# Branch norms and the pooling mixer interleaved with the last four units of the input projection and the first of the merge, in a streaming encoder step

## The reference

```
qa, ka, va, ub, cq, ckv, kpe, ud, gate_in = split_cols(h @ lw['w_in'])
q = (rmsnorm(cq, lw['c_q_norm']) @ lw['w_uq'])          # C: latent attention, query latent
ckv = rmsnorm(ckv, lw['c_kv_norm'])                     # C: key/value latent
ud = ud[..., :CONV_WIDTH] * jax.nn.sigmoid(ud[..., CONV_WIDTH:])
o_a = swa(qa, ka, va)                                   # A: sliding window attention
o_b = pool_mix(ub)        # B: trailing means over 2, 4, 8, 16 tokens, minus u, times w_pool, times a gain
o_c = mla(q, ckv, kpe)
o_d = silu(layernorm(conv31(ud)))                       # D: causal depthwise convolution of 31 taps
merged = sum over b of sigmoid(gate_b) * (o_b @ w_o_b)
x += merged @ w_out;  x += swiglu(rmsnorm(x))
```

## Time and profile before

| | us |
|---|---|
| median of 3 runs | 2405.38 (2404.38 to 2407.51) |
| profiled execution, its own time | 2410.11 |
| its span from the first to the last instruction | 2408.3 |
| PE busy (share) | 2270.8 (94%) |
| DVE, POOL, ACT busy | 1302.2, 949.3, 860.8 |
| mean granted TensorE clock | 0.981 of full |

### The profile page before, as it was taken

The page is one execution under the profiler, slowest core; times in us unless marked ns, Lnnn a source line. Parts: engine busy times, 40 slices in busy tenths (PEclk is TensorE's granted clock), DMA queues, the critical chain, the costliest instruction groups (busy, mean ns, idle before and its releaser), DMA issues.

```text
span 2408.3 us, 39646 instructions
## 1 busy us (share of the span) xinstructions
PE 2270.8 (94%) x14968; PEld 2179.9 (91%) x14968; DVE 1302.2 (54%) x2344; ACT 860.8 (36%) x1676; POOL 949.3 (39%) x988
## 2 busy tenths in 40 slices
PE   5997999999999999999989979999999989999996
PEld 5996999788999999999889969988889989999996
DVE  6996243333347835727389752533332487275364
ACT  2014333444314534526311152334442245254352
POOL 3552455232464332323445425542326623333331
PEclk9999999999999999999999989999999999999998
DMA  5241222011232221222224302211112312223221
GB/s 183 84 161 52 68 71 65 29 40 40 81 103 79 71 92 67 97 66 79 96 94 138 114 34 66 70 53 40 40 36 92 109 62 88 79 79 97 67 79 57
DMA packets 70417, 187.79 MB, mean 78 GB/s; under 512 B 19680, under 2 KB 22336, under 8 KB 69248
## 3 DMA queue, kind: packets, MB, share of 16 engines
q1 hardware_dynamic: 53536, 163.27, 20.7%
q10 hardware_dynamic: 16736, 22.52, 2.8%
HBM read 173.46 MB, written 14.14 MB: 78 GB/s over the span
## 4 chain that ended last, share of the span: by engine, by line
PE 87%; DVE 8%; issue 2%; ACT 2%; ACTq 0%; DMA 0%; SPq 0%; DVEq 0%
PE gemm L640 43%; PE gemm L1051 17%; PE gemm L1041 14%; PE side L1051 3%; PE side L924 2%; PE side L904 1%; DVE rstd L1607 1%; DVE act_lo L2034 1%; PE side L710 1%; PE side L855 1%; PE side L911 1%; DVE prod L1636 1%; DVE prod L1790 1%; PE side L782 1%; DVE x L1793 1%
## 5 line engine op out<-in xcount | busy, mean ns | idle before, releaser
L620 POOL TENSOR_TENSOR ring_lo<-w_raw,ring_hi 128x512 fp32r<-128x512 f32 x232 | 307.8, 1329 | 590.7 <-ACT ring_hi L1469 590.7
L603 POOL CAST w_hi<-w_raw 128x384 fp32r<-128x384 f32 x376 | 212.1, 564 | 803.1 <-PE gemm L640 783.7
L640 PE MATMUL gemm<-h_hi,w_hi 128*128 128x320 f32 x1728 | 431.2, 331 | 21.7 <-DVE h_lo L1613 17.0
L605 POOL TENSOR_TENSOR w_lo<-w_raw,w_hi 128x384 fp32r<-128x384 f32 x376 | 432.7, 1151 | 30.1
L640 PE MATMUL gemm<-h_hi,w_lo 128*128 128x320 f32 x1728 | 395.6, 310 | 0.0
L640 PE MATMUL gemm<-h_lo,w_hi 128*128 128x320 f32 x1728 | 395.5, 310 | 0.0
L640 PEld LDWEIGHTS gemm<-h_hi,w_hi 128*128 128x128 f32 x1728 | 294.3, 190 | 53.4 <-issue 39.5
L1051 PE MATMUL gemm<-act_hi,ring_hi 128*128 128x320 f32 x960 | 299.9, 312 | 18.9 <-issue 10.0
L1051 PE MATMUL gemm<-act_hi,ring_lo 128*128 128x320 f32 x960 | 299.1, 312 | 0.0
L1051 PE MATMUL gemm<-act_lo,ring_hi 128*128 128x320 f32 x960 | 299.0, 311 | 0.0
L640 PEld LDWEIGHTS gemm<-h_hi,w_lo 128*128 128x128 f32 x1728 | 290.6, 189 | 0.0
(11 more groups left out here) (276 smaller groups left out, 4168.8 us busy)
## 6 DMA issues: line engine op xcount, KB each, us to landing
w_raw<-in_ws_ff SPq DMA_DIRECT2D x120, 512.0 KB, 3.3
w_raw<-in_ws_gate SPq DMA_DIRECT2D x64, 512.0 KB, 3.3
w_raw<-in_ws_in SPq DMA_DIRECT2D x44, 512.0 KB, 3.3
w_raw<-in_ws_proj SPq DMA_DIRECT2D x64, 256.0 KB, 2.6
w_raw<-in_ws_out SPq DMA_DIRECT2D x16, 512.0 KB, 3.3
w_raw<-in_ws_fd SPq DMA_DIRECT2D x16, 384.0 KB, 3.0
x_park<-x ACTq DMA_DIRECT2D x2, 2560.0 KB, 12.7
x<-x_park ACTq DMA_DIRECT2D x4, 1280.0 KB, 5.8
```

Of the source, the lines that this page charges most:

```text
L603: eng.tensor_copy(w_hi[s][:, cols], w_raw[s][:, cols]).then_inc(w_high.sem, 1)
L605: eng.tensor_tensor(w_lo[s][:, cols], w_raw[s][:, cols], w_hi[s][:, cols].bitcast(F32), ALU.subtract).then_inc(w_split.sem, 1)
L620: eng.tensor_tensor(lo, src, hi.bitcast(F32), ALU.subtract).then_inc(lo_plain.sem, 1)
L640: mm = eng.matmul(dst[:, hf, 0:HALF], w, r[:, k, cols], start=first and k == 0 and part == 0, stop=last and k == kk - 1 and part == 2)
```

## The change

It moves the side work. TensorE's units 18 to 21 leave the loop and are written tile by tile, with the side work between tiles; DVE's and ACT's orders follow; the bank list changes with them. Pool scratch and the four pool results move to slices 2 to 7 of `macc` (the memory of x, which is parked in HBM by then), so that pool results no longer share `rstd` and the squares no longer share the partial sums' buffers. The seven stores move from ACT's queue to SP's, behind the cache loads and ahead of the load of unit 22. The core of the diff:

```
-        pw0p, pw1p, pws, pld = sq0, sq1, t2b, rstd
+        pws = t2b
+        pw0p, pw1p, pld = macc[:, 2, :], macc[:, 3, :], [macc[:, 4 + g, :] for g in range(4)]
 SyncE, after the load of kpe_cache, before the merge loads:
+                read_unit(eng, l, 16)
+                read_unit(eng, l, 17)
+                (five stores of kT, vT, kTs; two of k_full and v_full to o_k_s and o_v_s)
 TensorE:
-                with eng.Fori(1, A_UNITS // 2) as i:
+                with eng.Fori(1, A_UNITS // 2 - 2) as i:
-                colsum("lnm", [y[:, t, :] for t in range(4)], lambda n: None)
-                for g in range(4):
-                    ... pool product g ...
-                    merge_tiles(0, 2 * g, 2 * g + 2)
-                colsum("ckvn", *sq_tiles(0, 1), square=True)
-                colsum("lnv", *sq_tiles(1, 4), square=True)
-                colsum("cqn", *sq_tiles(5, 2), square=True)
-                merge_tiles(0, 8, 12)
-                merge_tiles(1, 0, 12)
+                unit_tiles(18, 0, KT)
+                unit_tiles(19, 0, 3)
+                evacuated(eng, l, ("conv", 3))
+                evacuated(eng, l, "convs")
+                for n in range(4):
+                    colsum("lnm", [y[:, t, :] for t in range(4)], n)
+                unit_tiles(19, 3, KT)
+                unit_tiles(20, 0, 1)
+                colsum("lnv", lnv, 0, 0)
+                colsum("lnv", lnv, 1, 0)
+                unit_tiles(20, 1, 3)
+                colsum("lnv", lnv, 2, 0)
+                unit_tiles(20, 3, 5)
+                colsum("lnv", lnv, 3, 0)
+                unit_tiles(20, 5, 7)
+                pool(0)
+                unit_tiles(20, 7, KT)
+                unit_tiles(21, 0, 3)
+                pool(1)
+                unit_tiles(21, 3, 6)
+                colsum("ckvn", sq_tiles(4, 1), 0, 4)
+                unit_tiles(21, 6, KT)
+                merge_tiles(0, 0, 5)
+                pool(2)
+                merge_tiles(0, 5, 7)
+                colsum("cqn", ..., 0, 5); colsum("cqn", ..., 1, 5)
+                merge_tiles(0, 7, 12)
+                merge_tiles(1, 0, 8)
+                pool(3)
+                merge_tiles(1, 8, 12)
 ScalarE, new order:
+   queries_out(0); squares of y 0, 1; queries_out(1); squares of y 2, 3; square of ckv;
+   stds("lnv"); pool(0); queries_out(2); square of cq 0; pool(1); four Silu and high parts;
+   queries_out(3); stds("ckvn"); square of cq 1; pool(2); merge_gate(0);
+   wait ckv_ready; stds("cqn"); store o_ckv; merge_gate(1); pool(3)
 VectorE, new order, behind the convolution:
+   pool(0); centre y 0 to 3; rotate kpe; pool(1); pool(2); reciprocal lnv; scale y 0 to 3;
+   o_lo 0 to 3; reciprocal ckvn, scale ckv; reciprocal cqn, scale cq 0, 1;
+   merge(0); pool(3); merge(1)
```

More of the change, by code:

```diff
@@ L70, in _bank_uses @@
     u += [(("lnm", h), 4 + h) for h in range(2)]
-    u += [(("pool", g, h), 6 + h) for g in range(4) for h in range(2)]
+    u += [(("lnv", h), 4 + h) for h in range(2)]
+    u += [(("pool", g, h), 6 + h) for g in range(2) for h in range(2)]
     u += [(("ckvn", h), 4 + h) for h in range(2)]
-    u += [(("lnv", h), 4 + h) for h in range(2)]
+    u += [(("pool", 2, h), 6 + h) for h in range(2)]
     u += [(("cqn", h), 4 + h) for h in range(2)]
+    u += [(("pool", 3, h), 6 + h) for h in range(2)]
     u += [(("kpe", h), 6 + h) for h in range(2)]
@@ L688, in _, with unit_tiles @@
                         products(l, i * 2 + s, G[s], s, KT, h_hi, h_lo)
+                def unit_tiles(u, first, last):
+                    for k in range(first, last):
+                        if k == 0:
+                            psum(u % 2, u // 2)
+                        product(l, u, G[u % 2], u % 2, k, KT, h_hi, h_lo)
                 def merge_tiles(n, first, last):
@@ L702, in merge_tiles @@
                             product(l, unit + 1, G[1], 1, t - KT, 4, o_hi, o_lo)
[L704 to L715, removed]
@@ L717, in sq_tiles, with colsum @@
-                def sq_tiles(first, n):
-                    return [sq[(first + k) % 2] for k in range(n)], \
-                        lambda k: eng.wait_ge(sq_ready.sem, sq_ready.at(l, first + k + 1))
+                def colsum(name, tiles, n, square=None):
+                    if square is not None:
+                        eng.wait_ge(sq_ready.sem, sq_ready.at(l, square + n + 1))
+                    for hf, cols in halves:
+                        if n == 0:
+                            fill(l, (name, hf))
+                        mm = eng.matmul(B[4 + hf][:, 0:HALF], ones[:, :], tiles[n][:, cols],
+                                        start=(n == 0), stop=(n == len(tiles) - 1))
+                        if n == len(tiles) - 1:
+                            mm.then_inc(side.sem, 1)
+                    if square is not None and n < len(tiles) - 1:
+                        mm.then_inc(sq_used.sem, 1)
@@ new lines, in sq_tiles, with pool @@
+                def sq_tiles(first, n):
+                    return [sq[(first + k) % 2] for k in range(n)]
+                def pool(g):
+                    eng.wait_ge(pooled.sem, pooled.at(l, g + 1))
+                    for hf, cols in halves:
+                        bank = fill(l, ("pool", g, hf))
+                        eng.matmul(bank[:, 0:HALF], wpl[:, g, :], pld[g][:, cols], start=True, stop=True)\
+                           .then_inc(side.sem, 1)
+                unit_tiles(18, 0, KT)
@@ L1234, in _, with queries_out @@
                 copy_unit(17, vT)
-                for t in range(4):
+                def queries_out(t):
                     g, free = take(18 + t)
@@ L1711, in _, with pool @@
                 eng.wait_ge(hist_zeroed.sem, hist_zeroed.at(l, 2))
-                step = 0
-                for g in range(4):
-                    src = (pbp[:, g, :], pbs[:, g, :, :])
+                eng.wait_ge(x_parked.sem, x_parked.at(l, 16))
+                def pool(g):
+                    step = sum(2 * (k + 1) + 3 for k in range(g))
+                    src, res = (pbp[:, g, :], pbs[:, g, :, :]), pld[g]
                     for lev in range(g + 1):
@@ L1755, in _ @@
                             ins.then_inc(ln_centred.sem, 1)
[L1757 to L1760, removed]
+                read_unit(eng, l, 13)
+                eng.tensor_tensor(kper[:, :], kper[:, :], cs[0:64, :], ALU.mult).then_inc(kpe_rot.sem, 1)
+                pool(1)
+                pool(2)
+                scaled(l, 1, lambda hf: ("lnv", hf))
                 for t in range(4):
```

95 lines of the change are left out of this document (50 added, 45 removed).

## The result

The changed kernel takes 2391.03 us (2388.87 to 2395.04, four runs), for 2405.53 (2404.38 to 2407.51) of the kernel before, timed beside it: a ratio of 0.9941, interval 0.9929 to 0.9954, or 14.5 us less. I had forecast 2388.5 and a gain of 16.9. The profiled execution took 2390.43 us, with a span of 2388.6.

The account below looks back on a forecast made before the run. TensorE bounds the kernel (87% of the chain), with 41.0 us wasted in two stretches. L745 at 77.5 instead of 85.0 and 86.9 gains 7.5 + 9.4 = 16.9: 2405.4 - 16.9 = 2388.5 us, range 2379 to 2400.

Parts of the forecast that it names:

- The convolution's end: After three tiles of unit 19, TensorE's LayerNorm sum waits for the convolution: a new stall of 2.0 us per layer.
- rival 2: More waits bite (cqn margin, clock at the convolution, lasting low clock): gain 5 to 9 us, 2398 us; chance 0.17.
- To the end of unit 22: TensorE's remaining tiles of units 19 to 22 and side work, up to merge 0's gate, end at 52.3 us.
- The chain to pool 3: From unit 22's end through ACT and DVE work: 16.4 us plus 2.1 of GpSimd contention, pool 3 ready at 70.9.
- The stall: TensorE runs out of tiles at 62.9 us and waits 8.0 us for pool 3 (5.9 to 9.8).
- The clock behind it: Lower TensorE clock after the wait for pool 3, up to L745: 2.0 us (bounds 0 and 4.6).
- To the rotary-key product: Pool 3's product 1.1 us, four tiles 3.5 and clock loss: L745 starts at 77.5 us after unit 18's start.
- The stores: SP issues seven stores in some 5 us before unit 22's load, issued near 169.6; 5 us slack, no cost taken.
- Rival 3: The stores choke the weights, so unit 22 comes late; at 20 us late, 2420 us; chance 0.07.
- Scratch in the accumulator: Removes the wait of pool g+1 for product g, letting DVE run ahead; its price is none.
- Rival 1: Stall at pool 3 much smaller, only the 2.0 us convolution wait left: gain 37.1 us, 2368 us; chance 0.1.
- rival 4: No change: the attention's first steps wait for cache loads or weights instead, within 0.2% of 2405; chance 0.06.

Follow-up runs that it names:

- filler: The changed kernel with 42 useless matmuls ahead of TensorE's wait for pool 3; 2387.52 us, ratio 0.9932.
- pool3_early: The changed kernel with DVE computing pool 3 ahead of the cq scaling instead of behind merge 0; 2391.24 us, ratio 0.9941.
- early_nolow: pool3_early without GpSimd's subtraction for the low weight parts, the high part multiplied instead (result not the reference's); 2374.77 us, ratio 0.9877.
- stores_act: The changed kernel with the seven stores back on ACT's queue, ahead of the copies of unit 18; 2394.03 us, ratio 0.9956.
- late_pool3: The changed kernel with TensorE's pool 3 multiplied behind the rotary-key product and first new-row transposes; 2375.71 us, ratio 0.9885.
- scratch_only: The kernel before with only pool scratch and results moved to the accumulator and its own wait removed, orders and stores unchanged; 2393.34 us, ratio 0.9961.

## Why the prediction was right, by its own steps

**The convolution's end: right in the wait, incomplete in its cost.** I forecast 2.0 us; 1.91 and 1.92 were measured. I gave the clock behind it no cost in the sum and put it into a rival. It falls in layer 1 of the changed kernel (6.24 us for 4.54, 1.7 us), in layer 1 of filler and of pool3_early, in layer 0 of early_nolow, in both layers of stores_act, and in neither of late_pool3. It is part of rival 2, and it is the term that the sum lacked.

**To the end of unit 22: right.** I forecast 52.3; ACT's sigmoid, released by it, starts at 209.57, which is 52.5. The thin margin at cqn held: no wait stands there.

**The chain to pool 3: right in its shape, one term wrong.** I forecast pool 3 ready at 70.9; it was ready at 69.9 (226.94). The term of 1.28 us for the sigmoid's table load behind the wait is wrong, since the load stands ahead of it. In the trace before it stood behind a wait for DVE, and I took that for a rule; this wait is for TensorE. Contention was forecast at 2.1 us and measured as 1.8 in pool 3 and 0.4 in cq's scaling, 2.2 together. The split of 235.74 that I cited for the reciprocal meets only its last tenth of a microsecond; that the reciprocal is untouched is shown by the changed kernel, where it takes 4.15 us (212.70) beside a subtraction of 1.02 us at 212.93.

**The stall: right.** I forecast 8.0 us (5.9 to 9.8) from 62.9 on; 6.91 and 6.97 were measured, from 63.1 on. Nearly all of the missing microsecond is the table load. late_pool3 shows that this wait and its clock are what separates 2391 from 2376, but for the 1.7 us of the convolution's clock in the profiled pair.

**The clock behind it: right in the mean.** I forecast 2.0 us; counted from 4.6 us for the product and four tiles at full speed it is 1.6 in layer 0 and 2.9 in layer 1, and filler takes it away.

**To the rotary-key product.** I forecast it at 77.5; it started at 76.1 and 79.2. Layer 0 is the table load and a smaller clock cost; layer 1 has 1.7 us from the convolution and 1.3 more behind pool 3. The two gains are 16.6 us together, for 16.9. That this is so close is partly luck. Layer 0 gained 1.4 us more than forecast and layer 1 1.7 less, from terms that have nothing to do with each other: a table load counted that wasn't there, a clock cost at the convolution left out. And the larger gain that I forecast for layer 1 rested on its longer stretch before (86.9 for 85.0 us), which was longer chiefly because the clock fell at the variance sum in that layer alone, 3.0 us (see scratch_only).

**The stores: right that they cost nothing, the working off.** SP's issues took 8.4 us and not 5, and the load of unit 22 went at 172.55 instead of 169.6; the slack of 5 us that I had estimated took it, as the wait at 182.63 shows. Rival 3 is refuted by stores_act.

**Scratch in the accumulator: priced wrongly as a step.** "Its price is none" was true as a cost and misleading as a share of the gain: alone it brings 10.6 us. The forecast of the time held since I had counted the whole stretch from the new order, without asking which edit gave it; as an account of where the gain comes from it was wrong.

**The sum.** The profiled executions differ by 19.7 us: 16.6 in the two stretches and 3.1 outside them (layer 0's unit 18 starts 0.8 earlier; 1.4 between the layers' stretches and 0.9 at the end). The medians differ by 14.5, since the profiled run of before was 4.6 above its median and that of the changed kernel 0.6 below. I had assumed the same difference for both. That was wrong and took away 5.2 us; the 3.1 outside the stretches, which I had not forecast either, gave part of it back, so that the median came out 2.5 us above the forecast. What the runs leave open is why the same 1.9 us wait lowers the clock in some layers and not in others, and the same 1.54 us wait in the kernel before. With 1.7 us each it could make 3.4 of the 6.2 us between the lowest and highest run of the changed kernel; that was argued from the sizes, not measured run by run.

Rival 1 is refuted (the stall is 6.9 us), rival 4 too (the attention keeps its distance of 6.65 us). Of rival 2, the clock at the convolution came true in one layer, and in part the low clock that lasts: in layer 1 the four tiles behind pool 3 took 5.0 us (granted clock 0.69) for 3.5.

## What to carry to other kernels

When side work is woven under matmuls, follow the longest chain of the other engines to its last result and put the tensor engine's use of it where that chain ends: here the weave left some 15 us at one product that could stand four tiles and a few transposes later. Before reordering, free the buffers: about two thirds of the gain came from results that no longer shared one. A wait on TensorE costs its length and, behind every wait of 5 us or more here and some of 1.5 to 2.2 us, slow matmuls too. A stretch of one trace holds such a clock loss or not by chance, so compare both layers before calling it waste. Moving a result on a contended engine earlier, beside a busy GpSimd, can lengthen it by more than it is moved.

## What the runs showed that I had not expected

- A wait of 1.9 us lowers TensorE's clock in some cases only: sixteen matmuls took 4.54 us or 6.24 behind the same wait, in layers of the same execution. In the kernel before it was 4.59 or 7.55 behind 1.54 us.
- Issuing one of the two stores from HBM to HBM took 3.76 us on SP in the changed kernel and the other 0.67; on ACT in stores_act they took 2.25 and 4.05. In layer 1 of stores_act they took 2.46 and 0.69, so which of the two is slow isn't fixed. Those of keys and values from SBUF took 0.6 to 1.0 each either way.
- ACT's table load went ahead of a wait for TensorE in the changed kernel (206.50, the wait ending at 209.57), though before it stood behind one for DVE. The next sigmoid's load in the changed kernel (219.80) stood behind a wait of 7.21 us for DVE again.
- Forty-two matmuls of no use in a wait brought the rotary-key product forward by 1.4 and 2.7 us behind it.
